# Retention of the first block in chunks of 128 tokens with a carried state, heads in pairs

## The reference

```
q, k   = rope(q, pos), rope(k, pos) * 64 ** -0.5
gamma  = 1 - 2 ** (-5 - h)                         (one number per head)
y[i]   = sum over j <= i of gamma ** (i - j) * (q[i] . k[j]) * v[j]
yn     = (y - mean(y)) / sqrt(var(y) + EPS)        (over the 128 of a head)
out    = silu(gate) * yn * g_gn
```

## Time and profile before

| | us |
|---|---|
| median of 3 runs | 2912.93 |
| lowest and highest | 2910.79 and 2915.97 |
| the profiled execution | 2909.04 |
| its span in the profile | 2907.3 |
| TensorE busy (7898 matmul records) | 2319.6 (80%) |
| VectorE busy | 1682.7 (58%) |
| ACT busy | 1020.4 (35%) |
| POOL busy | 704.2 (24%) |
| mean granted TensorE clock | 0.892 of full speed |

### The profile page before, as it was taken

How to read it: one execution, slowest core, us unless ns; L and a number is a source line. 1 busy time by engine, 2 the same in 40 slices (tenths; PEclk the granted TensorE clock), 3 DMA queues, 4 the chain that set the end, 5 groups by cost and what they waited for, 6 DMA issues and landing times. The chain is left out here.

```text
span 2907.3 us, 25668 instructions
## 1 busy us (share of the span) xinstructions
PE 2319.6 (80%) x7898; PEld 1404.1 (48%) x7898; DVE 1682.7 (58%) x3368; ACT 1020.4 (35%) x2504; POOL 704.2 (24%) x625
## 2 busy tenths in 40 slices
PE   6999898889718877787775777766777777699988
PEld 5778565467612222232222334422334563588877
DVE  5552434653486787877645676665666643455534
ACT  4123103532303333333333334443843443433322
POOL 1000202200104444344433444443444100100000
PEclk9999756899869989899997999978988887799999
DMA  6763200012109999999997999998999521322122
GB/s 217 221 185 96 67 0 4 22 56 68 67 35 422 421 387 421 389 414 421 395 421 299 421 420 421 419 399 326 361 389 421 164 58 44 103 101 101 72 76 98
DMA packets 142238, 684.95 MB, mean 236 GB/s; under 512 B 19169, under 2 KB 35713, under 8 KB 73489
## 3 DMA queue, kind: packets, MB, share of 16 engines
q0 software_dynamic: 73728, 536.90, 45.2%
q1 hardware_dynamic: 68384, 146.56, 15.5%
HBM read 681.30 MB, written 2.10 MB: 235 GB/s over the span
## 5 line engine op out<-in xcount | busy, mean ns | idle before, releaser
L1649 PE MATMUL peer_Y<-peer_w,peer_diag 128*128 128x512 f32 x1792 | 908.6, 643 | 246.4 <-ACT peer_diag L1635 229.6
L1593 POOL DMA_INDIRECT peer_w<-in_peer_uv,peer_eidx x512 | 588.8, 1150 | 860.3 <-PE peer_Y L1649 514.2
L1603 DVE CUSTOM_DVE_ANT_0 peer_junk<-peer_w,peer_xtok 128x1024 f32<-128x1024 f32 x512 | 623.2, 1225 | 281.5 <-DMA peer_w<-in_peer_uv,peer_eidx 255.2
L1649 PEld LDWEIGHTS peer_Y<-peer_w,peer_diag 128*128 128x128 f32 x1792 | 337.3, 202 | 763.8 <-ACT peer_diag L1635 465.0
L1627 ACT ACTIVATE peer_gel<-peer_dots 128x1 f32<-128x1 f32 x512 | 103.7, 203 | 753.1 <-DVE peer_dots L1603 751.0
L1635 ACT ACTIVATE peer_diag<-all_ident,peer_a 128x128 f32<-128x128 f32 x448 | 179.8, 401 | 15.5 <-PE peer_Y L1649 0.9
L1629 ACT ACTIVATE peer_a<-peer_gel,peer_gates 128x1 f32<-128x1 f32 x512 | 150.8, 294 | 16.6
L2127 PE MATMUL ffn_acc<-m2f_hs,ffn_cut 128*128 128x512 f32 x352 | 138.1, 392 | 9.4 <-DVE ffn_cut L2175 9.4
L2128 PE MATMUL ffn_acc<-m2f_hs,ffn_cut 128*128 128x512 f32 x352 | 137.7, 391 | 0.0
L2129 PE MATMUL ffn_acc<-m2f_hs,ffn_cut 128*128 128x512 f32 x352 | 137.7, 391 | 0.0
L651 DVE TENSOR_TENSOR p_cut<-m1h_raw,p_cut 128x512 fp32r<-128x512 f32 (+2 forms) x96 | 63.2, 660 | 128.4 <-ACT p_cut L677 128.4
(11 more groups left out here) (460 smaller groups left out, 4004.5 us busy)
## 6 DMA issues: line engine op xcount, KB each, us to landing
m_gates<-in_w_ada SPq DMA_DIRECT2D x48, 512.0 KB, 4.1
m2f_raw<-in_w_up SPq DMA_DIRECT2D x22, 1024.0 KB, 4.8
m1h_raw<-in_w_in SPq DMA_DIRECT2D x80, 256.0 KB, 3.1
m20h_raw<-in_w_in SPq DMA_DIRECT2D x48, 256.0 KB, 3.8
m22h_raw<-in_w_in SPq DMA_DIRECT2D x48, 256.0 KB, 3.3
m_down_ring<-in_w_down SPq DMA_DIRECT2D x22, 512.0 KB, 5.9
peer_w<-in_peer_uv,peer_eidx POOLq DMA_INDIRECT x512
m_out_ring<-in_w_out SPq DMA_DIRECT2D x16, 512.0 KB, 8.9
```

The costliest lines, as they stand in the source:

```text
L1593: pool.indirect_dma_start(self.w[:, n % self.RW].rearrange("p c n -> p (c n)"), None, self.uv_dram, bass.IndirectOffsetOnAxis(self.col(sel ...
L1603: dve.tensor_tensor_reduce(self.junk[:, n % 2, :], self.w[:, n % self.RW, 0, :], self.xtok[:, n // PICKS, :], 1.0, 0.0, ALU.mult, ALU.add, ...
L1649: ins = pe.matmul(self.Y[:, h, :], self.diag[:, i % self.RD, :], self.w[:, n % self.RW, 1, h * BANK:(h + 1) * BANK], start=(k == 0), stop= ...
```

## The change

The decay gamma ** (i - j) is split into a factor of the query, gamma ** (i + 1), and one of the key, gamma ** -(j + 1) times 64 ** -0.5, which VectorE multiplies in after the rotation, in place, as a third operation of each job. What is left of the decay table is a causal mask of 128x128. The four tiles of tokens are then handled in order, all eight heads at once: scores only within the tile, even heads from rows 0 to 63 into one bank and odd heads from rows 64 to 127 into the other; values as one product for each head; the part of earlier tiles and of the meta tokens as one product for each head with a state of 64x128, which accumulates in one PSUM bank `K` (two heads above each other) and which ACT copies out for each tile. `K` starts with the meta tokens' product. ACT now normalises the odd heads. The output turns and the gates go in halves of four heads and pieces of 128 columns. The two decay tables and their loads go; three small tables (ret_q, ret_k, ret_mask) join `ret_tables`, loaded at the end of `project`. The phase has 20 semaphores. In the diff, runs of removed lines longer than four are left out, since the old functions stand above.

```diff
@@ -62,12 +62,13 @@
     p = np.arange(P)[:, None].astype(np.float64)
 
     gamma = 1.0 - 2.0 ** (-5.0 - np.arange(RET_H))
...
+    at = np.full((5, P), -1.0)
+    at[:NT] = np.arange(SEQ).reshape(NT, P)
+    at[NT, :META] = np.arange(META) - META
+    power = lambda x: (gamma[None, None, :] ** x[:, :, None]).transpose(1, 0, 2).astype(np.float32).copy()
+    out["c_ret_q"] = power(at[:NT] + 1)
+    out["c_ret_k"] = (power(-(at + 1)) * np.float32(RET_DK ** -0.5)).copy()
+    out["c_ret_mask"] = (np.arange(P)[:, None] <= np.arange(P)[None, :]).astype(np.float32)
 
     col = np.arange(KEYS)[None, :]
     delta = META + 3 * P + p - col
@@ -934,167 +935,241 @@
                 side.scalar(act, u)
 
 
-def retention(nc, consts, rq, rk, rv, rgT, gain, rope, decay_dram, decay_meta_dram, early):
+def retention(nc, consts, rq, rk, rv, rgT, gain, tables, early):
 
     ident = consts["ident"]
     H = RET_H
     with Phase(nc, "ret") as ph:
-        decay = ph.sb("decay", [P, H, SEQ])
-        decay_m = ph.sb("decay_m", [META, H, SEQ])
+        rope, fq, fk, causal = (tables[n] for n in ("rope_ret", "ret_q", "ret_k", "ret_mask"))
         a = ph.sb("a", [P, 2, BANK])
         b = ph.sb("b", [P, 2, BANK])
...
+        qT = ph.sb("qT", [P, 2, 4, P])
+        kT = ph.sb("kT", [P, 2, 4, P])
+        m = ph.sb("m", [P, 2, 2, 4, P])
+        st = ph.sb("st", [P, 2, 4, RET_DV])
+        yn = ph.sb("yn", [P, 2, H, RET_DV])
+        stats = ph.sb("stats", [P, H, 6])
+        mv = ph.sb("mv", [P, NT, H, 2])
+        var = ph.sb("var", [P, NT, H])
+        rstd = ph.sb("rstd", [P, NT, H])
+        shift = ph.sb("shift", [P, NT, H])
+        S = ph.ps("S", [P, 2, BANK])
         Y = ph.ps("Y", [P, 2, BANK])
...
+        K = ph.ps("K", [P, BANK])
+        T = ph.ps("T", [P, 3, BANK])
+        names = ("early_landed", "cosed", "swapped", "roped", "decayed", "turned", "copied", "scored", "masked", "updated", "stated", "pv",
+                 "meaned", "rooted", "shifted", "even_normed", "odd_normed", "yturned", "gated", "dve_link")
+        (early_landed, cosed, swapped, roped, decayed, turned, copied, scored, masked, updated, stated, pv, meaned, rooted, shifted,
+         even_normed, odd_normed, yturned, gated, dve_link) = (ph.sem(n) for n in names)
+
+        jobs = [(rq, fq, 0, P), (rk, fk, NT, META), (rk, fk, 0, P)]
+        for t in range(1, NT):
+            jobs += [(rq, fq, t, P), (rk, fk, t, P)]
+        jobs_of = lambda t: (0, 1, 2) if t == 0 else (2 * t + 1, 2 * t + 2)
+        made_q = lambda t: 1 if t == 0 else 2 * t + 2
+        made_k = lambda t: 2 * t + 3
         heads = lambda x: x.rearrange("p (h e) -> p h e", e=RET_DK)
+        pair = lambda h: slice(64 * (h % 2), 64 * (h % 2) + 64)
+        out_of = lambda h: Y[:, h % 2, (h // 2) * P:(h // 2 + 1) * P]
+
+
+        uses, freed = {}, []
+        for t in range(-1, NT + 1):
+            if t + 1 < NT:
+                uses["q", t + 1], uses["k", t + 1] = len(freed), len(freed) + 1
+                freed += [(copied, 2 * t + 3), (copied, 2 * t + 4)]
+            if t >= 1:
+                uses["y", t - 1] = len(freed)
+                freed += [(gated, 2 * t - 1), (gated, 2 * t)]
+        bank_of = lambda u: T[:, u % 3, :]
         block = ph.straight()
 
         @block.sync
         def _(sp):
-            sp.dma_start(decay[:], decay_dram).then_inc(tables, 16)
-            sp.dma_start(decay_m[:], decay_meta_dram).then_inc(tables, 16)
             load_early(sp, early_landed, early)
 
         @block.gpsimd
         def _(pool):
...
+            def swap(t):
+                for i in jobs_of(t):
+                    src, _, n, rows = jobs[i]
+                    x, o = heads(src[0:rows, n, :]), heads(b[0:rows, i % 2, :])
+                    if i >= 2:
+                        pool.wait_ge(roped, i - 1)
+                    e = RET_DK // 2
+                    for lo, hi in ((0, e), (e, 0)):
+                        ins = pool.tensor_tensor(o[:, :, lo:lo + e], x[:, :, hi:hi + e], bc(rope[0:rows, n, 1, lo:lo + e], 1, H), ALU.mult)
+                    ins.then_inc(swapped, 1)
+
+            swap(0)
+            swap(1)
+            for t in range(NT + 1):
+                if t + 2 < NT:
+                    swap(t + 2)
+                if t >= 1:
+                    pool.wait_ge(meaned, t)
+                    pool.tensor_tensor(rstd[:, t - 1, :], var[:, t - 1, :], consts["half"][:, 0:H], ALU.pow).then_inc(rooted, 1)
 
         @block.vector
         def _(dve):
             link = Link(dve, dve_link)
...
+
+            def turn_phase(t):
+                for i in jobs_of(t):
+                    src, factor, n, rows = jobs[i]
+                    x, o, f = heads(src[0:rows, n, :]), heads(a[0:rows, i % 2, :]), factor[0:rows, n, :]
+                    dve.tensor_tensor(o, x, bc(rope[0:rows, n, 0, :], 1, H), ALU.mult).then_inc(cosed, 1)
+                    dve.wait_ge(cosed, i + 1)
+                    dve.wait_ge(swapped, i + 1)
+                    dve.tensor_tensor(a[0:rows, i % 2, :], a[0:rows, i % 2, :], b[0:rows, i % 2, :], ALU.add).then_inc(roped, 1)
+                    dve.wait_ge(roped, i + 1)
+                    dve.tensor_tensor(x, o, bc(f, 2, RET_DK), ALU.mult).then_inc(decayed, 1)
+
+            def mask(t):
+                dve.wait_ge(scored, t + 1)
+                if t >= 2:
+                    dve.wait_ge(pv, t - 1)
+                for odd in range(2):
+                    ins = dve.tensor_tensor(m[:, t % 2, odd], S[:, odd, :].rearrange("p (c i) -> p c i", i=P), bc(causal[:], 1, 4), ALU.mult)
+                ins.then_inc(masked, 1)
+
+            def moments(t):
+                dve.wait_ge(pv, t + 1)
+                for h in range(H):
+                    ins = dve.bn_stats(stats[:, h, :], out_of(h))
                 link(ins)
-                for n in range(NT):
-                    ins = dve.bn_aggr(mv[:, h, n, :], stats[:, n, :])
+                for h in range(H):
+                    ins = dve.bn_aggr(mv[:, t, h, :], stats[:, h, :])
                 link(ins)
...
+                dve.tensor_scalar(var[:, t, :], mv[:, t, :, 1], EPS, None, ALU.add).then_inc(meaned, 1)
+
+            def normalise(t):
+                dve.wait_ge(rooted, t + 1)
+                dve.scalar_tensor_tensor(shift[:, t, :], mv[:, t, :, 0], -1.0, rstd[:, t, :], ALU.mult, ALU.mult).then_inc(shifted, 1)
+                if t >= 2:
+                    dve.wait_ge(yturned, 2 * (t - 1))
+                for h in range(0, H, 2):
+                    ins = dve.tensor_scalar(yn[:, t % 2, h, :], out_of(h), mv[:, t, h, 0:1], rstd[:, t, h:h + 1], ALU.subtract, ALU.mult)
+                ins.then_inc(even_normed, 1)
+
+            def gate(t):
+                for half in range(2):
+                    dve.wait_ge(yturned, 2 * t + half + 1)
+                    for j in range(4):
+                        h = 4 * half + j
+                        dst = rgT[:, h, t * P:(t + 1) * P]
+                        ins = dve.scalar_tensor_tensor(dst, bank_of(uses["y", t] + half)[:, j * P:(j + 1) * P], gain[:, h:h + 1], dst, ALU.mult, ALU.mult)
+                    ins.then_inc(gated, 1)
+
+            turn_phase(0)
+            turn_phase(1)
+            for t in range(NT + 2):
+                if t < NT:
+                    mask(t)
+                if 1 <= t <= NT:
+                    moments(t - 1)
+                if t >= 2:
+                    gate(t - 2)
+                if 1 <= t <= NT:
+                    normalise(t - 1)
+                if t + 2 < NT:
+                    turn_phase(t + 2)
 
         @block.scalar
         def _(act):
-            for i, (src, t, rows, dst, col) in enumerate(jobs):
-                act.wait_ge(turned, i + 1)
-                act.activation(dst[:, :, col:col + rows], T[:, i % 2, :].rearrange("p (c q) -> p c q", q=P)[:, :, 0:rows], ACT.Copy).then_inc(copied, 1)
+            def copy(dst, use, made):
+                act.wait_ge(turned, made)
+                act.activation(dst, bank_of(use).rearrange("p (c q) -> p c q", q=P), ACT.Copy).then_inc(copied, 1)
+
+            def normalise(t):
+                act.wait_ge(shifted, t + 1)
+                if t >= 2:
+                    act.wait_ge(yturned, 2 * (t - 1))
+                for h in range(1, H, 2):
+                    ins = act.activation(yn[:, t % 2, h, :], out_of(h), ACT.Identity, bias=shift[:, t, h:h + 1], scale=rstd[:, t, h:h + 1])
+                ins.then_inc(odd_normed, 1)
+
+            for t in range(NT):
+                if t >= 2:
+                    normalise(t - 2)
+                    act.wait_ge(pv, t - 1)
+                copy(qT[:, t % 2], uses["q", t], 2 * t + 1)
+                copy(kT[:, t % 2], uses["k", t], 2 * t + 2)
+                act.wait_ge(updated, t + 1)
+                act.activation(st[:, t % 2], K[:].rearrange("p (c e) -> p c e", e=RET_DV), ACT.Copy).then_inc(stated, 1)
+            for t in range(NT - 2, NT):
+                normalise(t)
 
```

(107 more changed lines are left out.)

83 lines of the change are left out of this document (removed).

## The result

The changed kernel takes 2825.49 us (median of 4 runs, 2823.04 to 2836.79), beside 2911.86 for the old one on the same chip. The ratio is 0.9711, with a 95% interval of 0.9681 to 0.9742. The profiled execution took 2836.79 us with a span of 2835.0.

A forecast was written before the change was run, and what follows sets the result against it. TensorE at clock 0.50 bounds the old retention heads; in the new stage the chain between engines sets the length. Stage ends 68.2 us earlier: 2909.04 - 68.2 = 2840.8, plus 3.9 to the median gives 2844.7 us; range 2829 to 2860.

The forecast's parts named there:

- front, to the first output: Stage start on VectorE and TensorE: five rotation jobs, turns and copy of k1, scores, values 0, state products; ends at 344.7.
- chunk 0 to 1: Output to output: moments, power, normalise, copies of q2 and k2, scores of chunk 2, values, state products; 15.9 us.
- chunk 1 to 2: Same chain with chunk 3's scores, VectorE also waiting for chunk 0's turn and gating it before normalising; 16.6 us.
- The edits costed at nothing: Moved decay-table loads, three small added tables, 20 semaphores instead of 16: claimed to add no time.
- TensorE at 1.2 GHz throughout: Forecast case for the retention stage: clock 0.50, all TensorE prices at that level, stage end 401.1; chance 0.52.
- the rise at the end of the old stage: Sign for full clock: TensorE's clock rose at 464 to 466 after two heads' values without scores between.
- GLA: Late stage with the same 64-row alternate-half products at clock 0.50, cited against TensorE getting its full clock.
- Less a microsecond for spread: Whole program: allowance below the full-clock case's 2830.2 us, setting the range's low end at 2829.
- the 3.9 us added: Whole program: profiled execution lies 3.9 under the median, so 2840.8 became 2844.7 us.
- No overlap: Rival, chance 0.10: half-array scores, state products and updates cost 0.43 us each; stage end 418.7, program 2862.3 us.
- Drain before every instruction: Rival, chance 0.01: TensorE drains before each retention instruction, 0.72 us each; stage 8.7 us longer, program 2921.6 us.
- Full clock: Rival, chance 0.33 full or partial: every TensorE term in the retention stage halved; stage end 386.6, program 2830.2 us.

## Why the prediction was wrong in size

**What held.** The new stage is a chain between four engines. Its links were forecast from rows of the old trace, and are these, from output to output (346.09, 359.72, 373.47, 385.60, last gate 395.23):

| part | forecast | measured |
|---|---|---|
| front, to the first output | 26.6 | 24.8 |
| chunk 0 to 1 | 15.9 | 13.6 |
| chunk 1 to 2 | 16.6 | 13.8 |
| chunk 2 to 3 | 13.3 | 12.1 |
| tail | 10.5 | 9.6 |
| stage | 83.0 | 74.0 |

Jobs of 3.0 us beside the swaps (331.64 to 334.63) and 2.1 after them are as forecast. That k1 is folded 16.4 us in (forecast 16.3) is in part luck: the first job took 5.5 us and not 4.2 (321.28 to 326.75), because its folded multiply took 2.44, and the job of the 16 meta rows took 2.0 and not 3.0. The third operation costs 0.69 with POOL idle, or when it starts just ahead of the next swap (334.02 against 334.06). The two that start beside a running swap end 0.5 to 0.6 us behind it, after 2.44 and 1.09 us. This agrees with the exclusive lock of the Trainium skill (SBUF — State Buffer, "SBUF: two separate sides"). Scores at 2.01 were forecast as 2.13. The edits costed at nothing cost nothing that shows.

**First step that failed: TensorE at 1.2 GHz throughout.** Values with state products were priced at 5.86 us. They took 4.52, 4.54, 4.47 and 5.75, together 4.2 less; and the turn of chunk 0, quicker at the higher clock, no longer delays the gates in the second link (0.5). That is 4.7 of the 9.0 us. The case was there as a rival with 0.33, full or partial, and the stage of 74.0 lies between its 68.5 and the forecast's 83.0. What weighed against it was "105 us of unbroken work went at 0.50", and that was read wrongly: a stretch of work with 16-row products in it was taken to speak for work without them. The change takes just these products out of the values. The forecast counted their removal as saved instructions, not as what would let the clock rise. Its own row for the rival, the rise at the end of the old stage, was the better sign. GLA was weak evidence against: TensorE was busy for only 4.58 of those 8 us.

**The terms that were mis-sized.** The other 4.3 us are small: POOL's power took 1.65 and not 2.01 (on the path in the first link), a gate 0.26 and not 0.31 (8 in 2.07 up to the next instruction, on the path in two links and the tail), scores 0.12 less a group, and handovers.

**Second step that failed: from the profiled execution to the median.** "Less a microsecond for spread" and the 3.9 us added set the low end at 2829. The rest of the program alone varies by 10 us between executions (2751 to 2761 over the profiles of all the kernels here), and with the stage as measured the forecast would have been 2844.7 - 9.0 = 2835.7. The 3.9 had no footing: the new profiled execution lies 11 above its median. Taking it away leaves 6.3 us, which no trace locates. So the 19.2 us between forecast and median are 9.0 in the stage (4.7 of them the clock), 3.9 from the offset and 6.3 that stay open. With the stage alone put right, the forecast would still have been 10.2 us above the median.

**The rivals.** No overlap (0.10) is ruled out: a pair's product costs 0.25. Its worth was put at 17.6 us and is 8, since the same-half price is 0.38 and not 0.43, and half of the groups run at 2.4 GHz. Drain before every instruction (0.01) didn't occur. Full clock, forecast at a stage of 68.5 us, is what filling the pauses gives: 66.7.

**Where the 77 us come from.** Padding alone, with the old algorithm, shortens the stage from 152 to 94 us and the median by 54.5. The chunks with a carried state bring it from 94 to 74, of which the pairs are 8. Taken in this order, three quarters of the stage's gain (58 of 77) and about two thirds of the median's come with the 16-row products made full, and the rest with the smaller amount of work; in another order the shares could differ. The Trainium skill (TensorE: Matmul & The Clock Gate, Part 1) has sustained activity release the throttle. The 128-row values of the padded kernel agree, since the clock rose some 5 us into them. Products of fewer rows disagree: 12.7 us of 64-row scores there, and 105 us of the old mixture, kept TensorE busy without a break at 0.50.

## What to carry to other kernels

When a busy TensorE shows a granted clock of 0.50, look for products of few rows in the group, and pad them to 128 with zeros as an experiment before the algorithm is changed: here a few lines gave 54.5 us, where the rewrite gave 82 to 86. A price of TensorE is valid only beside the clock that the new mixture of work will get, so forecast both levels and ask which instructions disappear. Judge a change in one stage by the stage's own length, since the rest of this program moves by 10 us from run to run.

## What the runs showed that was not expected

- A mixture of 16-row and 128-row values and 64-row scores ran at 1.2 GHz (0.50) over 105 us without idle time. With the 16 rows filled up to 128 by zeros it was 2.4 GHz for 38 us on end, 64-row scores included. Why few rows have this effect isn't shown, and sizes between 16 and 64 weren't tried.
- 64-row scores did not lower the clock once it was up (1.00), but 12.7 us of them, unbroken, did not raise it either (0.50).
- Useless products in TensorE's pauses shortened the stage from 74.2 to 66.7 us, though they delay nothing and feed nothing.
- Updates of 64 columns in alternate halves of one bank overlap at 2.4 GHz: 0.13 us each, 0.19 with the same half in a row.
- The first folded multiply took 2.44 us beside POOL's swap, a later one 1.09 beside it, and the others of 128 rows 0.69.
